# A fused encoder step on one core: the second feed-forward product by one level of Strassen's method, with weight sums made by accumulating DMA

## What is computed

```python
x = x + rmsnorm(m @ w_out, g_mix_post)
h = rmsnorm(x, g_ffn_pre)
z = jnp.square(jax.nn.relu(h @ w_ff1))      # (384, 2048) @ (2048, 8192)
return x + rmsnorm(z @ w_ff2, g_ffn_post)   # (384, 8192) @ (8192, 2048)
```

## Time and profile before

| | |
|---|---|
| median of 3 runs | 1959.03 us (1958.05 to 1959.9) |
| the profiled execution | 1959.6 us |
| its span | 1958.0 us |
| mean granted TensorE clock | 0.995 |
| busy: TensorE, VectorE, ScalarE, GpSimd | 1931.4, 857.1, 663.4, 196.2 us |
| DMA | 269.45 MB, mean 138 GB/s |

### The profile page before, as it was taken

One profiled execution on the slowest core, in us unless ns is written; L12 is line 12 of the kernel. 1 busy time (PEld: TensorE's weight loads), 2 busy tenths in 40 slices (PEclk: granted clock), 3 DMA queues, 4 the chain that ended last, 5 costly groups with the idle time before them and its releaser, 6 DMA issues.

```text
span 1958.0 us, 26741 instructions
## 1 busy us (share of the span) xinstructions
PE 1931.4 (99%) x10594; PEld 1783.3 (91%) x10594; DVE 857.1 (44%) x1118; ACT 663.4 (34%) x934; POOL 196.2 (10%) x245
## 2 busy tenths in 40 slices
...
GB/s 199 126 133 190 189 198 153 209 121 127 129 130 125 124 128 224 167 61 145 124 129 128 129 121 127 131 120 139 120 129 129 129 124 126 127 129 129 127 126 81
DMA packets 210465, 269.45 MB, mean 138 GB/s; under 512 B 15345, under 2 KB 138449, under 8 KB 209456
## 3 DMA queue, kind: packets, MB, share of 16 engines
...
...
## 4 chain that ended last, share of the span: by engine, by line
PE 97%; DVE 1%; ACT 0%; DMA 0%; issue 0%; DVEq 0%; SPq 0%; ACTq 0%
PE ps L504 19%; PE ps L506 19%; PE ps L505 19%; PE ps L531 12%; PE ps L530 12%; PE ps L532 12%; PE ps L684 1%; PE ps L750 0%; PE ps L701 0%; PE ps L672 0%; PE ps L755 0%; PE ps L542 0%; PE ps L711 0%; PE ps L720 0%; PE ps L657 0%; DMA x_sb<-in_x_prompt_dram 0%
## 5 line engine op out<-in xcount | busy, mean ns | idle before, releaser
L1478 DVE TENSOR_TENSOR w_lo<-w_raw,w_hi 128x1024 fp32r<-128x1024 f32 x426 | 532.4, 1251 | 811.2 <-ACT w_hi L1018 807.9
L1018 ACT CAST w_hi<-w_raw 128x1024 fp32r<-128x1024 f32 x426 | 446.7, 1050 | 856.0 <-PE ps L506 439.7
L504 PE MATMUL ps<-ht_hi,w_hi 128*128 128x384 f32 x2000 | 675.8, 338 | 5.0 <-DVE ht_lo L1523 3.4
L506 PE MATMUL ps<-ht_hi,w_lo 128*128 128x384 f32 x2000 | 669.7, 335 | 0.0
L505 PE MATMUL ps<-ht_lo,w_hi 128*128 128x384 f32 x2000 | 669.5, 335 | 0.0
L504 PEld LDWEIGHTS ps<-ht_hi,w_hi 128*128 128x128 f32 x2000 | 376.1, 188 | 6.9 <-DVE ht_lo L1523 3.6
L505 PEld LDWEIGHTS ps<-ht_lo,w_hi 128*128 128x128 f32 x2000 | 376.3, 188 | 1.2 <-issue 0.8
L506 PEld LDWEIGHTS ps<-ht_hi,w_lo 128*128 128x128 f32 x2000 | 376.0, 188 | 0.0
L531 PE MATMUL ps<-w_lo,z_hi 128*128 128x512 f32 x762 | 300.3, 394 | 0.0
L530 PE MATMUL ps<-w_hi,z_hi 128*128 128x512 f32 x762 | 298.7, 392 | 0.0
L532 PE MATMUL ps<-w_hi,z_lo 128*128 128x512 f32 x762 | 296.0, 388 | 0.0
...
## 6 DMA issues: line engine op xcount, KB each, us to landing
w_raw<-in_w_ff_dram SPq DMA_DIRECT2D x256, 512.0 KB, 3.7
w_raw<-in_w_in_dram SPq DMA_DIRECT2D x130, 512.0 KB, 7.4
w_raw<-in_w_out_dram SPq DMA_DIRECT2D x32, 512.0 KB, 3.8
kc<-in_cache_k_dram POOLq DMA_DIRECT2D x8, 1024.0 KB, 11.5
vc<-in_cache_v_dram POOLq DMA_DIRECT2D x8, 1024.0 KB, 11.3
w_raw<-in_w_attn_up_dram SPq DMA_DIRECT2D x16, 512.0 KB, 3.6
...
x_sb<-in_x_prompt_dram SPq DMA_DIRECT2D x2, 1024.0 KB, 6.0
```

Source lines behind the costliest of these rows:

```text
L504: pe.matmul(out, wh[:, k, cols], x_hi[:, kk, :], start=(kk == 0), stop=False)
L506: last = pe.matmul(out, wl[:, k, cols], x_hi[:, kk, :], start=False, stop=(kk == k_last))
L1018: nc.scalar.copy(w_hi[:, u % RING, :], w_raw[:, u % RAWS, :]).then_inc(hi_ready, 1)
L1478: nc.vector.tensor_tensor(w_lo[:, u % RING, :], w_raw[:, u % RAWS, :], f32(w_hi[:, u % RING, :]), ALU.subtract).then_inc(lo_ready, 1)
```

## The change

In chunks 0 to 6 the second product goes by one level of Strassen's method in Winograd's form. The 2 x 2 blocks are row tiles 0 and 1, the even and odd k-blocks of 128, and two neighbouring column groups of 512. A half of the chunk's columns (`pair` 0 or 1, two column groups) now takes 14 right-hand sides, in the order `RHS`: six stored weight units (B12 is never used by itself) and eight sums T1 to T4, each for two sets `_0`, `_1` of k-blocks. Row tile 2 uses the same right-hand sides (C31 and E). A right-hand side is a unit: it is cast, subtracted and used as before, for one or two products of 6 matmuls (`product`), so that a half has 22 products where it had 24.

The sums are made by GpSimd's DMA queue, with `accum_op=ALU.add`, in the raw slots themselves: T3 = B22 + B12 from DRAM onto B22's slot once B22 is converted; T1 = B12 + B11 from DRAM onto B12's slot; T2 = B11 + T3 from slot to slot; T4 = B21 + T2 from slot to slot. There are now 12 raw slots (six more, `x_raw`, where the residual lay), and a slot is loaded again only when its sum has been converted. The residual is stored to DRAM and loaded back during chunk 7.

The row sums are made by VectorE (`row_sums`), five blocks for each pair of z blocks, cast and subtracted like z (`zb_hi`, `zb_lo`, 10 blocks of 128 columns). The products are kept in 18 accumulators of 512 columns; VectorE adds each PSUM bank to its own (`evict`, 18 per chunk, a copy in chunk 0), and in chunk 7 sixteen additions (`total`) turn them into the output's blocks. Chunk 7 itself is computed as before.

The diff, cut to its core:

```diff
+ROLES = ("B22_0", "B12_0", "B12_1", "B11_0", "B21_0", "B22_1", "B11_1", "B21_1")
+RHS = ("B22_0", "B11_0", "B21_0", "B22_1", "B11_1", "B21_1", "T3_0", "T3_1",
+       "T1_0", "T2_0", "T1_1", "T2_1", "T4_0", "T4_1")
+SUMS = ("T3_0", "T1_0", "T1_1", "T3_1", "T2_0", "T2_1", "T4_0", "T4_1")
+FREED = {"B22": "T2", "B12": "T1", "B11": "T4", "B21": "T4"}
+PRODUCTS = {"B11": (("Q1", A11), ("C31", A31)), "B22": (("Q3", S4),), "B21": (("Q2", A12), ("C31", A32)),
+            "T3": (("Q7", S3),), "T1": (("Q5", S1), ("E", S5)), "T2": (("Q6", S2),), "T4": (("Q4", A22), ("E", A32))}
+CLOSED = {"Q3": 3, "Q1": 4, "Q2": 5, "C31": 5, "Q7": 7, "Q5": 10, "Q6": 11, "E": 13, "Q4": 13}
...
+            def load_x(c0, r, lap, src, k, w):
...
+                    sp.wait_ge(lo_ready, freed(c0, r - XRAWS) + lap * (3 * CONVS))
...
+                sp.dma_start(dst.rearrange("p (k w) -> p k w", w=w), src).then_inc(landed, 16)
...
+            def product(cb, more, idx, pair):
...
+                for q, blk in PRODUCTS[kind]:
+                    out = ps[:, Q_BANK[pair][q], :]
+                    for k in range(2):
...
+                        pe.matmul(out, zb_hi[:, pr, blk, :], wh[:, k, :], start=begins, stop=False)
+                        pe.matmul(out, zb_hi[:, pr, blk, :], wl[:, k, :], start=False, stop=False)
+                        last = pe.matmul(out, zb_lo[:, pr, blk, :], wh[:, k, :], start=False, stop=ends)
+                last.then_inc(unit_used, 1)
...
+                for idx in range(14):
+                    if idx == 0:
+                        pe.wait_ge(zs_lo, c * 4 + (2 if c0 else 3))
+                    elif idx == 1:
+                        pe.wait_ge(za_lo, c * 4 + (2 if c0 else 3))
+                    elif idx == 3:
+                        pe.wait_ge(zs_lo, c * 4 + 4)
+                    elif idx == 4:
+                        pe.wait_ge(za_lo, c * 4 + 4)
...
+                    product(cb, more, idx, 0)
...
+            def row_sums(done, z, steps):
...
+                nc.vector.tensor_tensor(s_f[:, 0:2, :], tiles[:, 0, 0:3:2, :], tiles[:, 1, 0:3:2, :],
+                                        ALU.subtract).then_inc(s_step, 1)
+                nc.vector.tensor_tensor(s_f[:, 3, :], tiles[:, 0, 0, :], tiles[:, 0, 1, :], ALU.subtract)
...
+                nc.vector.tensor_tensor(s_f[:, 2, :], tiles[:, 0, 1, :], s_f[:, 0, :],
+                                        ALU.subtract).then_inc(s_step, 1)
...
+                nc.vector.tensor_tensor(s_f[:, 4, :], tiles[:, 1, 1, :], s_f[:, 2, :],
+                                        ALU.subtract).then_inc(s_done, 1)
...
+                    for k in range(16, CONVS + 1):
+                        if k < CONVS:
+                            convert(c0, lap, k + 2)
+                        if k == 17:
+                            sums_lo(c, 3, 3)
+                        for pair in range(2):
+                            done = k - 1 - 16 - 14 * pair
+                            for q in EVICTED:
+                                if CLOSED[q] == done:
+                                    dve.wait_ge(unit_used, cb + 16 + 14 * pair + done + 1 + lap * (3 * CONVS))
+                                    evict(c0, pair, q)
...
+            def weight_sum(c0, lap, c, pair, n):
...
+                if kind == "T3":
+                    converted("B22")
+                    dst, src = slot_of("B22"), stored("B12")
+                elif kind == "T1":
+                    pool.wait_ge(raw("B12")[1], raw("B12")[2] + lap * (96 // XRAWS * 16))
+                    dst, src = slot_of("B12"), stored("B11")
+                elif kind == "T2":
+                    converted("B11")
+                    summed("T3")
+                    dst, src = slot_of("B11"), slot_of("B22")
+                else:
+                    converted("B21")
+                    summed("T2")
+                    dst, src = slot_of("B21"), slot_of("B11")
...
+                pool.dma_start(dst, src, accum_op=ALU.add).then_inc(sum_landed[n], 16)
```

More of the change, by code:

```diff
@@ L158, in streaming_encoder @@
     ybuf = place("ybuf", [P, TT, D], F32, ATT)
+    acc_a = place("acc_a", [P, 12, 512], F32, ATT)
     f_x = place("f_x", [H, T], F32, ATT)
@@ new lines, in chunk @@
+            def chunk(c0, lap, c):
+                for pr in range(4) if c0 else range(2, 4):
+                    for q in range(4):
+                        src = wff1_v[:, 4 * q:4 * q + 4, bass.ds(c * CHUNK + 256 * pr, 256)]
+                        if c0 == 0:
+                            load(U_FFN + 4 * pr + q, 0, src, 4, 256)
+                        else:
+                            load_x(c0, 4 * pr + q, lap, src, 4, 256)
+                for r in range(16):
+                    if c0 == NCHUNK - 1:
+                        cg, q = divmod(r, 4)
+                        src = wff2_v[:, bass.ds(c * 8 + 2 * q, 2), 512 * cg:512 * cg + 512]
+                    else:
+                        pair, m = divmod(r, 8)
+                        kind, half = ROLES[m].split("_")
+                        cg = 2 * pair + int(kind[2]) - 1
+                        src = wff2_h[int(kind[1]) - 1][:, bass.ds(c * 4 + 2 * int(half), 2), 512 * cg:512 * cg + 512]
+                    load_x(c0, 16 + r, lap, src, 2, 512)
@@ new lines, in chunk @@
+            def chunk(c0, lap, c):
+                cb, more = U_FFN + CONVS * c0, lap * 22
+                is_last = c0 == NCHUNK - 1
+                if c0 == 0:
+                    first_up()
+                for pr in range(4) if c0 else range(2, 4):
+                    if c0:
+                        if pr == 0:
+                            pe.wait_ge(o_added, c * 18 - 4)
+                        elif pr == 1:
+                            pe.wait_ge(o_added, c * 18 - 1)
+                        else:
+                            pe.wait_ge(relu_ready, c * 4 + (pr - 1))
@@ L997, in _ @@
-            chunk(U_FFN, 0, 0)
+                if is_last:
+                    for cg in range(4):
+                        banks = [[4, 5, 6], [7, 0, 1]][cg % 2]
+                        if cg == 0:
+                            pe.wait_ge(o_added, c * 18)
+                        elif cg == 1:
+                            pe.wait_ge(relu_ready, c * 4 + 4)
+                        else:
+                            pe.wait_ge(o_added, c * 18 + 3 * (cg - 1))
+                        for tiles in ((0,), (1,), (2,)) if cg == 3 else ((0, 1, 2),):
+                            for q in range(4):
+                                if cg == 0:
+                                    pe.wait_ge(za_lo, c * 4 + (q + 1))
+                                down(cb + 16 + 4 * cg + q, 0, banks, 2 * q, z_hi, z_lo,
+                                     CHUNK // P - 1, o_psum, tiles)
+                    return
@@ L998, in _ @@
+                for idx in range(14):
+                    if idx in (0, 1, 2, 6, 8, 9, 12):
+                        pe.wait_ge(o_added, c * 18 + {0: 3, 1: 4, 2: 5, 6: 6, 8: 8, 9: 9, 12: 11}[idx])
+                    product(cb, more, idx, 1)
+            chunk(0, 0, 0)
             with pe.Fori(0, 2) as i:
                 for j in range(3):
-                    chunk(U_FFN + 32 * (1 + j), i * 16, i * 3 + (1 + j))
-            chunk(U_FFN + 32 * (NCHUNK - 1), 0, NCHUNK - 1, True)
+                    chunk(1 + j, i, i * 3 + (1 + j))
@@ L1004, in _ @@
+            chunk(NCHUNK - 1, 0, NCHUNK - 1)
         @block.scalar
```

462 lines of the change are left out of this document (319 added, 143 removed).

## The result

| | before | after |
|---|---|---|
| median of the runs, us | 1958.62 (1958.05 to 1959.90, 4 runs) | 1978.91 (1975.93 to 1979.92, 4 runs) |
| profiled execution, us (span) | 1959.6 (1958.0) | 1979.92 (1978.3) |
| mean granted clock | 0.995 | 0.986 |

The change makes the kernel slower by 20 us: the ratio is 1.0100, with an interval of 1.0083 to 1.0118. The forecast was 1934 us, faster. The sign is that of rival (a), at less than half of its size (20 us where it had 47).

The account below looks back on a forecast made before the run. The prediction took TensorE, busy 99% of the span, as the bound: 1959.6 - 38.5 (matmuls) + 9.1 (turn) + 3.5 (weight sums) = 1933.7, say 1934 us. The forecast's own range was 1926 to 1946; the 8-in-10 range reached to 2035.

Parts of the forecast that it names:

- rival (a): GpSimd's queue: sums T3_1, T2_1, T4_1 come late, 11 us a chunk, kernel slower at 2007 us; chance 0.32.
- The matmuls: Second product, seven chunks: 24 fewer matmuls each at 0.229 us, 38.5 us less.
- The turn: From up to down, before unit 18: TensorE waits some 1.3 us for VectorE, seven times, +9.1 us.
- The four widths without a row: VectorE's work at the turn: 0.41 us for 256 columns, 0.28 for 128, 0.82 for 640, estimated from other rows.
- The small hand-overs: Short units, tightest at T1_0: fits by 0.2 us, taken as nothing; bounds 0 and 0.5 us at two places a chunk.
- the accumulators: Products' accumulators: their place, and sixteen additions in chunk 7 at 0.68 us each, hidden and taken as nothing.
- the spill: Residual stored to DRAM and reloaded: taken as nothing.
- GpSimd's issue: GpSimd's issuing of the sums: 0.53 us each, 8.5 of 127 us, taken as nothing.
- Rival (b): Hand-overs of VectorE and ScalarE leave gaps in short units, about 1 us per half: 1944 us; chance 0.10.
- The weight sums: Sixteen accumulating DMAs a chunk: 5.0 us each to landing, late by 0.5 us a chunk, +3.5 us.
- The argument against (a): Against late sums: the DMA engines are idle 60% of a chunk.
- point of decision: Late sums decide the sign from 2.1 us per half (29.4 / 14), at about 3.0 us an add.

Follow-up runs that it names:

- e1: The changed kernel with none of the weight sums issued, the sum units being converted from unsummed slots (output incomplete): 1931.34 us, ratio 0.9858.
- e2: The changed kernel with each sum adding only 128 of its 512 columns, a quarter of the bytes (output incomplete): 1931.15 us, ratio 0.9857.
- e3: The changed kernel with the same transfers as plain copies that overwrite the slot, without the addition (output incomplete): 1929.90 us, ratio 0.9854.
- e9: The changed kernel with SyncE's loads for the next chunk held until T4_0 of the second half before has landed: 1959.61 us, ratio 0.9995.
- e11: The changed kernel with only GpSimd's queue order changed, both T1 sums ahead of T3_0: 1979.99 us, ratio 1.0118.
- e5: The changed kernel with two plain copies for each add, to the slot and to spare DRAM (output lacks the sums): 2001.56 us, ratio 1.0212.
- e13: The changed kernel with the next chunk's loads held for T4_0 and both T1 sums first in GpSimd's queue: 1936.91 us, ratio 0.9889.

## Why the prediction was wrong, and where it was right

- **The matmuls: right.** 7 x 24 x 0.229 = 38.5 us. In e1 a chunk is 128.15 us, that is 132.51 less 5.50 plus 1.1 for the turn, and the whole kernel is within 1.2 us of the forecast without its term for the sums (1931.3 against 1930.2).
- **The turn: right, slightly less.** TensorE's idle there is 0.83 us in the changed kernel, seven times 0.8 in e1; by the chunk's length it costs 1.1, not 1.3. The four widths without a row measured 425 ns (256 columns; 0.41 taken), 284 to 292 (128 columns; 0.28), 817 (640 columns; 0.82).
- **The small hand-overs, the accumulators, the spill, GpSimd's issue: right as nothing.** e1, e2 and e3 leave TensorE no wait but the turn's and one of 2.2 to 2.5 us at the loop's edge. Rival (b) is out.
- **The weight sums: the step that failed**, forecast +3.5 us, measured +47.6. T3_1 was to land before ScalarE wanted it, and it landed 3.9 us too late for TensorE. The overlap that it counted on was not there, and two numbers in it were wrong. The engines' time of an add was taken as 2.6 us (a second read's 1.3 at the busiest rate, on top of 1.3); it is 2.9 to 3.0. The other was that at most one load of SyncE might share the engines, and that SyncE's loads cost nothing beyond.

  Counted from the first of the four issues at 1118.5: 1.2 for the issue, four adds of 3.0, and the 1.1 that the prediction has behind them are 1132.8; measured is 1136.1, and the 3.3 between are two loads' time (39.6% of the engines x 850 us / 206 loads = 1.6 each), or in part T2_0's, issued at 1128.67. That split is an estimate. e9 speaks for it: with the next chunk's loads held, the same count from 1250.73 gives 1265.0 for T3_1 of chunk 2, and its cast starts at 1265.22, although T2_0 had been issued at 1258.10.

  TensorE needed it at 1132.2 (1134.6, less 2.4 for cast and residue). By this count it would have landed at 1131.2 at 2.6 and with no load, in time by 1.0; at 3.0 and with no load, 0.6 late; as it was, 3.9 late. Each of the two numbers looked harmless against 1.0 us of room.
- **The lower clock was in no term and in no rival.** A stall of 3.9 us costs 6.7. Of the 47.6 us, 19 are this.
- **The argument against (a) was an average.** "The DMA engines are idle 60% of a chunk" is true, 0.40. But 13 of the 16 sums are issued in the 60 us of the down phase, where the share is 0.89 to 1.04, and the other three just ahead of it; the window should have been cut at the turn before it was used.
- **Rival (a) had the mechanism and the place, with too high a price.** T3_1 of the second half of chunk 1 lands 16.8 us after the half's first product (1119.3), where (a) had 14.6, and TensorE waits 3.9 us for it, where it had 3.6; that these two agree is partly luck, since it counted from 11.0, when ScalarE could take the unit, and TensorE needs it by 12.9. The other sums lose less than its 4 and 3: over all, 4.1 us of waiting a chunk and 2.7 of clock, where it had 11 of waiting. So 1979 and not 2007. Its point of decision, about 3.0 us an add for 29.4 us, was near, but at 2.9 to 3.0 the loss was already 47.6: the loads and the clock came on top.
- **The loop's edge** costs 4.0 us in e1 (132.19 against 128.15) and cost 1.4 before. The trace of e1 has 2.24 us of waiting there and then eleven matmuls of 384 columns up to 0.32 us apart, not 0.17, at the lower clock, 1.7 us more: 3.9 in all.

```profile
1400.00:1402.00 2.00, 2.00 (x8) 2.00 (x7) 0.00 (x0) 1.04 (x1) 0.00 (x0) 0.50 1.10 348
```

- **Open:** where that wait comes from; one of 2.2 to 4.2 us stands there in every experiment but e11, and not in the changed kernel. Open too are the 22 us by which e5 exceeds the adds, and the 6 us that e13 is above e1.
